# One core, two transformer blocks: the attention's transposes one take later, scores and values side by side

## The reference

```
s = jnp.einsum('bnqkgd,bnskd->bnkgqs', qb, kw) * ATT_SCALE
s = jnp.where(mask[None, :, None, None, :, :], s, NEG_INF_2)
p = jax.nn.softmax(jnp.concatenate([s, sink], axis=-1), axis=-1)[..., :-1]
o = jnp.einsum('bnkgqs,bnskd->bnqkgd', p.astype(v.dtype), vw)
```

## Time and profile before

| | |
|---|---|
| median of three runs | 1066.82 us (1065.77 to 1070.26) |
| span of the profiled execution, first to last instruction | 1060.6 us |
| TensorE busy | 1019.7 us, 96% |
| VectorE, ScalarE busy | 846.2 us, 658.2 us |
| the chain that ended last | TensorE 70%, VectorE 15%, ScalarE 8% |

### The profile page before, as it was taken

How to read it: one execution, slowest core, us unless ns; L and a number is a source line. 1 busy time by engine, 2 the same in 40 slices (tenths; PEclk the granted TensorE clock), 3 DMA queues, 4 the chain that set the end, 5 groups by cost and what they waited for, 6 DMA issues and landing times.

```text
span 1060.6 us, 16486 instructions
## 1 busy us (share of the span) xinstructions
PE 1019.7 (96%) x6099; PEld 872.7 (82%) x6099; DVE 846.2 (80%) x1663; ACT 658.2 (62%) x1323; POOL 50.7 (5%) x48
## 2 busy tenths in 40 slices
PE   6989999999999999999989999999999999999997
PEld 4867888887888888888868989888887988888986
DVE  5878877778999999999959667797658876598584
ACT  6454646547888898888834676732445467762352
POOL 0201100002001020020000000000100000000010
PEclk9999999999999999999989999999999999999999
DMA  8533345342999999999935333333344433233321
GB/s 341 196 121 118 120 166 193 120 159 81 385 380 357 395 372 366 393 341 386 371 138 180 139 140 140 116 123 120 120 178 179 160 120 136 104 136 142 105 95 40
DMA packets 30179, 211.33 MB, mean 199 GB/s; under 512 B 3728, under 2 KB 3856, under 8 KB 5136
## 3 DMA queue, kind: packets, MB, share of 16 engines
q1 hardware_dynamic: 28368, 205.01, 51.6%
q10 hardware_dynamic: 1728, 5.21, 1.4%
HBM read 209.16 MB, written 1.05 MB: 198 GB/s over the span
## 4 chain that ended last, share of the span: by engine, by line
PE 70%; DVE 15%; ACT 8%; DMA 3%; issue 3%; POOL 0%; ACTq 0%; DVEq 0%; POOLq 0%; SPq 0%
PE ps L529 19%; PE ps L531 18%; PE ps L530 18%; DVE w_lo L409 6%; PE ps L1006 5%; PE ps L534 4%; DMA ring<-in_panels 2%; PE ps L689 2%; ACT w_hi L1926 2%; PE ps L720 1%; ACT s_buf L1972 1%; DVE s_buf L412 1%; DMA g_in<-in_prm 1%; PE ps L998 1%; PE ps L744 1%
## 5 line engine op out<-in xcount | busy, mean ns | idle before, releaser
L409 DVE TENSOR_TENSOR w_lo<-ring,w_hi 128x512 fp32r<-128x512 f32 x760 | 482.1, 691 | 82.7 <-ACT w_hi L1926 81.4
L1926 ACT ACTIVATE w_hi<-ring 128x512 fp32r<-128x512 f32 x760 | 425.6, 621 | 157.2 <-PE ps L531 124.7
L529 PE MATMUL ps<-w_hi,op_rows 128*128 128x512 f32 (+2 forms) x800 | 316.7, 396 | 7.9 <-DVE op_rows L409 3.8
L531 PE MATMUL ps<-w_hi,op_rows 128*128 128x512 f32 (+2 forms) x800 | 310.0, 388 | 0.0
L530 PE MATMUL ps<-w_lo,op_rows 128*128 128x512 f32 (+2 forms) x800 | 308.9, 386 | 0.0
L529 PEld LDWEIGHTS ps<-w_hi,op_rows 128*128 128x128 f32 x800 | 152.1, 190 | 39.9 <-issue 7.5
L531 PEld LDWEIGHTS ps<-w_hi,op_rows 128*128 128x128 f32 x800 | 151.6, 190 | 31.4
L530 PEld LDWEIGHTS ps<-w_lo,op_rows 128*128 128x128 f32 x800 | 152.3, 190 | 28.0
L529 PE MATMUL ps<-op_rows,w_hi 128*128 128x256 f32 x544 | 157.4, 289 | 0.0
L530 PE MATMUL ps<-op_rows,w_hi 128*128 128x256 f32 x544 | 153.8, 283 | 0.0
L531 PE MATMUL ps<-op_rows,w_lo 128*128 128x256 f32 x544 | 153.7, 283 | 0.0
(11 more groups left out here) (243 smaller groups left out, 1055.5 us busy)
## 6 DMA issues: line engine op xcount, KB each, us to landing
ring<-in_panels SPq DMA_DIRECT2D x194, 1024.0 KB, 6.0
cst<-in_c ACTq DMA_DIRECT2D x1, 1229.0 KB, 7.3
buf_a<-in_pre ACTq DMA_DIRECT2D x2, 512.0 KB, 5.9
keys<-in_post ACTq DMA_DIRECT2D x2, 512.0 KB, 4.6
out<-x_tok SPq DMA_DIRECT2D x2, 512.0 KB, 2.6
cst<-in_c ACTq DMA_DIRECT2D x1, 960.0 KB, 6.8
x_tok<-in_x SPq DMA_DIRECT2D x1, 512.0 KB, 4.7
x_tok<-in_x ACTq DMA_DIRECT2D x1, 512.0 KB, 4.9
```

Of the source, the lines that this page charges most:

```text
L409: return V.tensor_tensor(o, a, b, op)
L529: T.matmul(o, l[0], r[0], start=start, stop=False)
L531: return T.matmul(o, l[1], r[0], start=False, stop=stop)
L1926: return A.activation(o, a, ACT.Copy, scale=scale)
```

## The change

Two lists in `at_ticks` are changed. Before, `turn` stood in its row's take, between `values` and `scores`, and `turn_out` at the take after. Now `turn` stands behind the take after its row's, and `turn_out` at the take after that, which is mostly the take of the next row. `weigh`, `values`, `scores` and their copies keep their takes. All 28 turns are moved. No instruction is added or removed.

```
     for take, scores, turn, values in rows:
-        for name, job in (("weigh", turn), ("values", values), ("turn", turn), ("scores", scores)):
+        for name, job in (("weigh", turn), ("values", values), ("scores", scores)):
             if job is not None:
                 table.setdefault(take, []).append((name, job))
-        for name, job in (("turn_out", turn), ("scores_out", scores), ("values_out", values)):
+        for name, job in (("scores_out", scores), ("values_out", values), ("turn", turn)):
             if job is not None:
                 table.setdefault(take + 1, []).append((name, job))
+        if turn is not None:
+            table.setdefault(take + 2, []).insert(0, ("turn_out", turn))
```

## The result

The changed kernel takes 1071.0 us (median of 7 runs, 1068.82 to 1074.31) against 1065.77 us for the kernel before (7 runs of the same session, 1061.9 to 1070.26). The ratio is 1.0051, with a 95% interval of 1.0033 to 1.0069: 5.4 us slower, 3.5 to 7.4 us. Forecast were 1076.3 us with a range of 1069.5 to 1081.0 us. The profiled execution took 1071.0 us with a span of 1069.2 us, so 1.8 us lie around the span. One of the twelve executions of e5 took 1949.19 us, in a slow state, and no ratio counts it.

A forecast was written before the change was run, and what follows sets the result against it. TensorE, busy 96% of the span, was taken as the bound. Two layers at +5.0 us and the first block at -0.5 us gave +9.5 us on 1066.8, 1076.3 us; 8 in 10 range 1069.5 to 1081.0 us.

The forecast's parts named there:

- my own case: Whole kernel: the clock falls in both layers, 1076.3 us, own range 1073 to 1080 us, chance 0.60.
- Part 1: TensorE's waits for VectorE's weighing before the transposes all go: 3.9 us in the first block, 1.35 us a layer.
- Part 2: New neighbours on TensorE gain 0.08 us per regular job: -0.8 us in the first block, -0.5 us a layer.
- Part 3: Values newly wait for ScalarE's `turn_out`: 1.2 us a layer, 4.2 us in the first block.
- Part 4: End of a layer's attention: the last `turn_out` slides behind `qf_on`, TensorE stands still 4.65 us, costing 3.35 us a layer.
- Part 5: After that stillness TensorE's clock falls to half in each layer, costing 2.3 us a layer (1.7 to 2.9).
- the clock holds, or falls once: Rival for the layers: no fall gives 1071.7 us, one fall 1074.0 us; chance 0.19.
- Faster: Rival at the recurrence's start: ScalarE and VectorE already pace it, so late TensorE loses nothing; -6.8 us, 1060.0 us, chance 0.06.
- transposes alone cool the clock: Rival: each of 28 lone turns lets TensorE's clock fall, 1.7 us each, 48 us, 1114 us; chance 0.03.

The follow-up runs named there:

- e5: The changed kernel with ScalarE making `turn_out` in front of the two weight copies of its take, not behind them: 1064.06 us, ratio 0.9986 to the kernel before.
- e2: The kernel before with only the last turn of each layer moved: 1074.2 us, ratio 1.0085 to the kernel before.
- e9: The kernel before with only `turn_out` put in front of its take's weight copies, every turn in its old place: 1065.15 us, ratio 1.0009.
- e6: The changed kernel with `turn_out` in front of the weight copies and each layer's last turn in its old place: 1055.75 us, ratio 0.9913 to the kernel before.
- e3: The kernel before with only the first block's turns moved: 1062.24 us, ratio 0.9974 to the kernel before.
- e4: The changed kernel with 18 unused products in front of the last values of each layer: 1068.88 us, ratio 1.0025 to the kernel before.
- e8: The changed kernel with each layer's last `turn_out` directly in front of the gates' activations, transposes still late: 1061.85 us, ratio 0.9965 to the kernel before.

## Why the prediction was right, point by point

The direction and the place were right, and the size was too large by 4.1 us (9.5 forecast, 5.4 measured, and at most 7.4 by the interval). The 1071.0 us lie outside the 1073 to 1080 us that I had given my own case, and below the 1072.1 us from which I would have called the kernel slower; that it is slower shows only against runs of the kernel before made beside it. The mechanism in the layers was as forecast; that the time came to lie inside the range of 8 in 10 is owed to the range's width as well.

The terms as the traces have them, in us; where the layers differ, layer 0 stands first:

| term | forecast | measured |
|---|---|---|
| first block, Part 1 | -3.9 | -3.9 |
| first block, Part 2 | -0.8 | -2.1 |
| first block, Part 3 | +4.2 | +2.2 |
| first block, the clock | 0 | +1.5 |
| first block | -0.5 | -2.3 |
| a layer, Part 1 | -1.35 | -1.3 |
| a layer, Part 2 | -0.5 | -0.9 |
| a layer, Part 3 | +1.2 | +1.5 |
| a layer, Part 4 | +3.35 | +3.1 |
| a layer, Part 5 | +2.3 | +2.4 and +1.5 |
| a layer | +5.0 | +4.8 and +3.9 |

Part 4 is e2's 5.54 us less its clock (8.97 us from the last values to `level` 0 in layer 0, against 6.50 us at full clock). Part 2 of a layer is what remains of the layer's sum. Part 3 of the first block is 4.2 us of new waits less 2.0 us of old ones that went.

- **Part 1, the wait before the transposes.** Right. The row is gone from the view. e9 shows that it stays without the late turns.
- **Part 2, the neighbours.** Right for a regular row, too small for the first block. I forecast a gain of 0.08 us for a regular job. Without its wait a regular row takes 8.51 - 0.20 = 8.31 us. Before, the same row took 8.40 us, from the values at 641.11 to those at 649.51. In the first block the distances from one group of values to the next, less the waits and the clock, shrank by 0.09 to 0.24 us each, 2.1 us together. The largest gains stand where a wait went or came, so part of them may be what a wait costs beside its idle time; no run parts the two.
- **Part 3, the new wait of the values, layers.** Four waits of 0.20 to 0.21 us stand where I had put 0.3 us. One of 0.70 us, at the first values of each layer, I had not seen. Together 1.5 us a layer, forecast 1.2 us. e5 and e6 show that it is the two weight copies: with the copy in front of them all of these waits vanish.
- **Part 3, first block.** The waits sum to 4.2 us, as forecast, but not where I put them: values 2 and 11 did not wait, values 6 and 10 waited 1.35 and 1.72 us. This is the term that was most mis-sized. I charged the waits nearly in full, and 2.0 us of other waits went in exchange. In the kernel before, the compression's products behind values 6, its transposes behind values 10, and values 11 themselves had waited:

```profile
142.15 3.67 PE L744 MATMUL ps<-ring,buf_d 128*64 128x256 f32 x32 [0.40 <-DVE buf_d L409]
186.72 0.60 PE L534 MATMUL ps<-ident,scr 128*64 128x128 f32 x4 [1.10 <-issue]
194.16 0.87 PE L720 MATMUL ps<-pt_buf,zin 128*64 128x256 f32 x8 [0.74 <-DVE zin L409]
```

  In the kernel after, the first two are 0.12 and 0.13 us and the third is gone. The stage shortened by 2.3 us (186.13 to 183.84) against 0.5 us forecast, and e3's total is 2.8 us faster. The clock also fell there, at 183.3 us, which I had not foreseen: the 24 products behind values 10 took 4.44 us where they had taken 2.92 us.
- **Part 4, the end of a layer's attention.** Right: 4.59 us of stillness against 4.65, at the instruction named. From the end of that wait to level 0 are 6.5 us at full clock (6.52 us in e4). It took 8.94 us (669.33 to 678.27), 2.4 us of it clock.
- **Part 5, the clock.** It fell in both layers, as forecast. It cost 2.4 us in layer 0. In layer 1 it was at half for 3.3 us and cost 1.5 us by e4, a little under my lower bound of 1.7 us; I had taken the mean of the two cases. From the first scores of the layer to level 0, layer 0 took 4.83 us more than before and layer 1 3.89 us, forecast 5.0 each. e2 measures Parts 4 and 5 alone, 5.54 and 5.76 us, forecast 5.65 each. One of the two falls that I took the price from, that at 801.7 us, did not cost it: from layer 0's level 0 to layer 1's first scores are 172.30 us with this fall, and 172.25 us in e9, which has the same instructions there and no fall. VectorE was busy for 3.33 of those 3.40 us. That it, and not TensorE, set the pace there is a guess; it is not shown.
- **Sum.** The terms as the trace has them are -2.3 + 4.8 + 3.9 = +6.4 us, inside the interval of the ratio. Of my error of 4.1 us, 1.8 us are the first block and 1.3 us the layers, mostly layer 1's clock. The other 1.0 us is covered by noise. The upper end of my range was also added up wrongly: the upper bounds of Parts 4 and 5 in one layer lead to 1078.6 us; the 1081.0 us that stand there take them in both. I had also put 6.2 us around the span. It is 1.8 us, and the other 4.4 us was the distance of a short execution from the median. It cancels in the difference.

Of the rivals, "the clock holds, or falls once" came nearest in time (1071.7 us), for a wrong reason: the clock fell twice. "Faster" was refuted by e2, and "transposes alone cool the clock" by e4 and e8, in which the late turns stand alone and the clock holds through the layers' attentions. The rule of the Trainium skill on transposes ("TensorE: Matmul & The Clock Gate", section "Part 4: PE-mode transpose") does not decide here: 0.58 us of them between two dense takes (661.06 to 661.64) cost no clock, which was 1.00 for 661 to 664.7 us.

## What to carry to other kernels

When a step moves by one slot, follow its partner on the other engine: the copy that the next consumer waits for can slide behind an unrelated long step of that engine's list. Look at the last job of a pipeline first, because other work is put there as soon as the pipeline thins out. Two of 28 moved steps cost more than the other 26 gained, and moving each with its copy's place in view made 9.3 us out of the same idea.

## What the runs showed of the hardware

- A single idle time can cost more than its length. After 4.59 us of stillness TensorE's clock was at half for 5.5 us, which added 2.4 us; filling the idle time with unused products held it at 1.00 (e4).
- The same wait can let the clock fall or not. Around the wait near 57 us, 1.95 us long, before kept its clock:

```profile
56.00:59.40 3.40, 1.45 (x10) 1.04 (x10) 3.12 (x6) 1.51 (x3) 0.00 (x0) 1.00 0.73 292
```

  and e6, with the same instructions up to there, lost it after 1.98 us (e2 and e5 lost it too, after 1.93 and 1.95 us):

```profile
55.60:59.00 3.40, 1.42 (x9) 0.77 (x7) 3.40 (x7) 2.49 (x5) 0.00 (x0) 1.00 0.74 263
59.00:62.40 3.40, 3.40 (x14) 2.49 (x12) 0.70 (x2) 0.00 (x0) 0.00 (x0) 0.50 0.82 253
```

- A fall of the clock can cost nothing. The one at 801.7 us in the kernel before lasted 3.4 us; between layer 0's level 0 and layer 1's first scores it is not to be seen. The five executions with a fall there took 172.24 to 172.31 us, the six without one 172.17 to 172.28 us.
- The expert stage, in which the page of the kernel after shows 346 to 414 GB/s, differs by up to 5.3 us between executions of the same instructions, as much as the whole effect. Why is open; a comparison of two single spans says little in this kernel.
